# Grouped attention by pairs of heads, with late tiles of q projected between its steps, and norm squares added on VectorE

## The reference

```python
def rmsnorm_2(x, g):
    return x * lax.rsqrt(jnp.mean(x * x, axis=-1, keepdims=True) + EPS) * g

def attention_mixer(h, w_qkv, w_o, q_gain, k_gain, cos, sin):
    G = N_HEADS // N_KV_HEADS                       # 16 heads, 4 kv heads, HEAD_DIM 64
    q, k, v = jnp.split(h @ w_qkv, [N_HEADS * HEAD_DIM, (N_HEADS + N_KV_HEADS) * HEAD_DIM], axis=-1)
    q = apply_rope(rmsnorm_2(q, q_gain), cos, sin)  # over the 64 of a head
    k = apply_rope(rmsnorm_2(k, k_gain), cos, sin)
    def block(q_blk):                               # 128 queries
        s = jnp.einsum('bqkgd,bskd->bkgqs', q_blk, k) * HEAD_DIM ** -0.5
        p = jax.nn.softmax(s, axis=-1)
        return jnp.einsum('bkgqs,bskd->bqkgd', p, v)
    return lax.map(block, qb).reshape(Bsz, L, N_HEADS * HEAD_DIM) @ w_o
```

## Time and profile before

| what | value |
|---|---|
| median of 3 runs | 3399.99 us (3398.29 to 3401.54) |
| the profiled execution | 3402.33 us, span 3400.1 us |
| busy, of the span | PE 3083.2 (91%), DVE 1417.6 (42%), POOL 1525.8 (45%), ACT 720.1 (21%) |
| last products of the first k tile to first scores | 1781 to 1871 us |
| head loop, to the first product of `gq_out` | 1871 to 2039.6 us |
| a GEMM tile with no ones matmul, 24 products | 5.44 us |

### The profile page before, as it was taken

How to read it: one execution, slowest core, us unless ns; L and a number is a source line. 1 busy time by engine, 2 the same in 40 slices (tenths; PEclk the granted TensorE clock), 3 DMA queues, 4 the chain that set the end, 5 groups by cost and what they waited for, 6 DMA issues and landing times.

```text
span 3400.1 us, 38788 instructions
## 1 busy us (share of the span) xinstructions
PE 3083.2 (91%) x14739; PEld 2403.7 (71%) x14739; DVE 1417.6 (42%) x1983; ACT 720.1 (21%) x1069; POOL 1525.8 (45%) x926
## 2 busy tenths in 40 slices
PE   8897899999887999999989889999989777699998
PEld 7885898788634877788866437888867344478886
DVE  5675655111234047433344552332066666433311
ACT  2373222433232000111013551111011111011100
POOL 5441322444203655565543014666555444456663
PEclk9997999999898999999999999999989788899999
DMA  3110000222100245556541002333222000123331
GB/s 111 62 63 32 1 0 0 63 74 74 38 0 25 99 161 182 165 173 188 192 133 62 0 13 62 99 90 102 93 64 101 16 16 16 50 75 99 98 103 59
DMA packets 291644, 259.51 MB, mean 76 GB/s; under 512 B 6329, under 2 KB 263958, under 8 KB 291276
## 3 DMA queue, kind: packets, MB, share of 16 engines
q1 hardware_dynamic: 287840, 248.53, 23.4%
q0 software_dynamic: 2256, 6.55, 0.6%
q10 hardware_dynamic: 1436, 2.96, 0.2%
HBM read 255.92 MB, written 2.10 MB: 76 GB/s over the span
## 4 chain that ended last, share of the span: by engine, by line
PE 78%; DVE 9%; issue 4%; ACT 3%; POOL 2%; DVEq 2%; DMA 1%; POOLq 1%; ACTq 0%; SPq 0%
PE ps L487 19%; PE ps L488 19%; PE ps L489 18%; DVE cv L1881 2%; PE ps L1377 2%; PE ps L1357 2%; PE ps L1453 2%; PE ps L1150 1%; PE ps L1163 1%; PE ps L578 1%; PE ps L1260 1%; PE ps L1169 1%; PE ps L692 1%; DVE HN L598 1%; PE ps L1270 1%
## 5 line engine op out<-in xcount | busy, mean ns | idle before, releaser
L487 PE MATMUL ps<-HNH,spl 128*128 128x512 f32 (+1 forms) x2496 | 914.5, 366 | 61.3 <-DVE HNL L591 24.2
L661 POOL TENSOR_TENSOR spl<-raw,spl 128x1024 fp32r<-128x1024 f32 (+1 forms) x352 | 894.5, 2541 | 55.3 <-issue 5.5
L488 PE MATMUL ps<-HNL,spl 128*128 128x512 f32 (+1 forms) x2496 | 899.3, 360 | 0.0
L489 PE MATMUL ps<-HNH,spl 128*128 128x512 f32 (+1 forms) x2496 | 895.7, 359 | 0.0
L659 POOL CAST spl<-raw 128x1024 fp32r<-128x1024 f32 (+1 forms) x352 | 390.5, 1109 | 1055.0 <-PE ps L489 974.5
L487 PEld LDWEIGHTS ps<-HNH,spl 128*128 128x128 f32 x2496 | 480.2, 192 | 160.9 <-issue 58.6
L488 PEld LDWEIGHTS ps<-HNL,spl 128*128 128x128 f32 x2496 | 480.6, 193 | 72.6 <-issue 4.3
L489 PEld LDWEIGHTS ps<-HNH,spl 128*128 128x128 f32 x2496 | 479.4, 192 | 69.7
L487 PE MATMUL ps<-AFH,spl 128*128 128x512 f32 x528 | 212.8, 403 | 0.0
L489 PE MATMUL ps<-AFH,spl 128*128 128x512 f32 x528 | 205.8, 390 | 0.0
L488 PE MATMUL ps<-AFL,spl 128*128 128x512 f32 x528 | 205.8, 390 | 0.0
(11 more groups left out here) (419 smaller groups left out, 4348.9 us busy)
## 6 DMA issues: line engine op xcount, KB each, us to landing
adw<-in_ada_w SPq DMA_DIRECT2D x96, 512.0 KB, 6.2
raw<-in_w_in SPq DMA_DIRECT2D x44, 1024.0 KB, 5.2
raw<-in_ffn_w_up SPq DMA_DIRECT2D x88, 512.0 KB, 4.8
raw<-in_w_ffn_in SPq DMA_DIRECT2D x44, 512.0 KB, 5.0
raw<-in_ffn_w_down SPq DMA_DIRECT2D x16, 1408.0 KB, 6.4
raw<-in_hy_w_in SPq DMA_DIRECT2D x12, 1024.0 KB, 5.1
raw<-in_w_ffn_out SPq DMA_DIRECT2D x8, 1408.0 KB, 6.8
raw<-in_w_branch_dn SPq DMA_DIRECT2D x8, 1024.0 KB, 5.1
```

Of the source, the lines that this page charges most:

```text
L487: pe.matmul(dst, w[0], x[0], start=first, stop=False)
L488: pe.matmul(dst, w[0], x[1], start=False, stop=False)
L489: return pe.matmul(dst, w[1], x[0], start=False, stop=final)
L661: pool.tensor_tensor(lo, w, hi, ALU.subtract).then_inc(split_ready, 1)
```

## The change

It has two parts that meet in the attention stage.

Norms (u=1 to 6; the first one, `norm_first_pe`, is as before): ACT writes the squares of tiles 1 to 6 into PSUM banks 1 and 3 in turn, those of tile 0 and 7 into the two buffers of `NSQ`. DVE adds each of the six to `NSQ` 0 (`norm_add`, called from `add_residual` behind the residual of the next tile, the last one ahead of the last tile's). PE makes two ones matmuls in place of eight, behind the whole GEMM.

Attention: the weights come in the order k, v, q. Ahead of the scores stand the k and v tiles and two of q (`AHEAD` = 4). The loop is written out as 32 steps e = 4p+j: pair p of heads (2p, 2p+1), which share a tile of `QG`, and block j of 128 queries. In step e PE computes the scores of step e+2 (two matmuls, one in each half of the partitions, straight from `QG` and `KDUP`) and transposes the two blocks of step e; weighted stands once a pair, at the first step of the next, as eight matmuls that take the two heads' column halves in turn, into bank 6. Pairs 0 to 5 each hold one of the six late q tiles: twelve products in step 1 and twelve in step 2, into bank 7, the sum in step 3, the rotation in step 0 of the next pair. POOL stages nothing; `OG` is gone, for DVE takes `OGL` from PSUM pair by pair.

```diff
@@ norms @@
+                if u:
+                    if k in (3, 4, 5, 6):
+                        act.wait_ge(n_add, (KD - 2) * (u - 1) + k - 2)
+                    dst = NSQ[:, k // (KD - 1), 0:n] if k in (0, KD - 1) else ps[:, 1 + k % 2 * 2, 0:n]
+                    act.activation(dst, x(k), ACT.Square).then_inc(n_sq, 1)
...
-        def norm_after(pe, u):
-
-            return lambda t: norm_pe(pe, u, SEQ, range(t - 1, t)) if t else None
+        def norm_pe(pe, u):
+            pe.wait_ge(n_add, (KD - 2) * u)
+            pe.matmul(ps[:, 6, :], ones[:, :], NSQ[:, 0, 0:SEQ], start=True, stop=False).then_inc(n_sum, 1)
+            pe.wait_ge(n_sq, KD * (u + 1))
+            pe.matmul(ps[:, 6, :], ones[:, :], NSQ[:, 1, 0:SEQ], start=False, stop=True).then_inc(n_sum, 1)
+
+        def norm_add(dve, u, k):
+            dve.wait_ge(n_sq, KD * u + k + 1)
+            dve.drain()
+            x = NSQ[:, 0, 0:SEQ]
+            dve.tensor_tensor(x, x, ps[:, 1 + k % 2 * 2, :], ALU.add).then_inc(n_add, 1)
...
-            def add_residual(gm, gate=None, before=None):
+            def add_residual(gm, u, gate=None, before=None):
...
+                    if t == KD - 1:
+                        norm_add(dve, u, t - 1)
                     b = acc_in(dve, gm, 0, t)
...
+                    if 2 <= t < KD - 1:
+                        norm_add(dve, u, t - 1)
@@ POOL @@
-            pool_split(pool, gq_k)
-            pool_split(pool, gq_q)
-            pool_split(pool, gq_v)
-            pool.wait_ge(a_done, 10)
-            pool.wait_ge(a_dupc, KVH)
...
+            for gm in (gq_k, gq_v, gq_q):
+                pool_split(pool, gm)
@@ PE, attention @@
+            def q_part(n, bank, ks):
...
+                    if n < AHEAD:
+                        pe.wait_ge(acc_free[gm.buf(t)], gm.free(t))
+                    else:
+                        pe.wait_ge(a_done, n)
+                for k in ks:
+                    mm = products(pe, ps[:, bank, :], halves_of(gm, t, k), x_hn(k), k == 0, k == KD - 1)
...
+            def scores(e):
+                p, q = e // NT, e % NT
+                if q == 0:
+                    pe.wait_ge(a_done, FIRST_Q + p + 1)
+                if e >= 2:
+                    pe.wait_ge(a_e, 2 * (e - 1))
+                for s in range(2):
+                    x = slice(s * HD, (s + 1) * HD)
+                    mm = pe.matmul(ps[:, e % 2 * 2 + s, :], QG[x, p, q * P:(q + 1) * P], KDUP[x, p // 2, :], start=True, stop=True)
+                mm.then_inc(a_s, 1)
+
+            def turn_over(e):
+                for s in range(2):
+                    i = 2 * e + s
+                    pe.wait_ge(a_p, i + 1)
+                    if i >= 2:
+                        pe.wait_ge(a_tc, i - 1)
+                    for kt in range(NT):
+                        mm = pe.transpose(ps[:, 4 + s, kt * P:(kt + 1) * P], PB[:, e % 2, s, kt * P:(kt + 1) * P], ident)
+                    mm.then_inc(a_t, 1)
+
+            def weighted(p):
+                pe.wait_ge(a_tc, 2 * NT * (p + 1))
+                if p:
+                    pe.wait_ge(split_x, NT + KD + p)
+                for kt in range(NT):
+                    for s in range(2):
+                        x = slice(s * HD, (s + 1) * HD)
+                        mm = pe.matmul(ps[x, 6, :], VG[:, kt, p // 2 * HD:(p // 2 + 1) * HD], PTB[:, p % 2, s, kt, :],
+                                       start=kt == 0, stop=kt == NT - 1)
+                mm.then_inc(a_o, 1)
...
+                if n and j in (1, 2):
+                    q_part(n, 7, range(4 * j - 4, 4 * j))
+                if n and j == 3:
+                    qk_sum(n)
+                turn_over(e)
+                if j == 0 and p and late_tile(e - 1):
+                    qk_rot(late_tile(e - 1))
+            weighted(PAIRS - 1)
@@ ACT, attention @@
+            for e in range(STEPS):
+                p, j, n = e // NT, e % NT, late_tile(e)
+                if n and j == 2:
+                    q_in(n)
+                turned(e)
+                if n and j == 3:
+                    qk_rs(n)
+                if e + 2 < STEPS:
+                    exps(e + 2)
+                if j == 0 and p:
+                    heads_hi(p - 1)
@@ DVE, attention @@
+            for e in range(STEPS):
+                p, j, n = e // NT, e % NT, late_tile(e)
+                shares(e)
+                if e + 2 < STEPS:
+                    maxima(e + 2)
+                if n and j == 3:
+                    q_norm(n)
+                if j == 0 and p and late_tile(e - 1):
+                    rope(late_tile(e - 1))
+                if j == 1 and p:
+                    heads_lo(p - 1)
```

More of the change, by code:

```diff
@@ new lines, in v_turn_over @@
+            def v_turn_over(t):
+                taken(pe, gq_v, 0, t)
+                for c in range(NT):
+                    mm = pe.transpose(ps[:, 4 + t, c * P:(c + 1) * P], PTB[:, 0, 0, t, c * P:(c + 1) * P], ident)
+                mm.then_inc(sv_t, 1)
+            def scores(e):
[8 more added lines that the diff above has]
+                mm.then_inc(a_s, 1)
@@ new lines, in turned, with heads_hi @@
+            def turned(e):
+                p, q = e // NT, e % NT
+                if q == 0 and p >= 2:
+                    act.wait_ge(a_o, p - 1)
+                for s in range(2):
+                    act.wait_ge(a_t, 2 * e + s + 1)
+                    act.activation(PTB[:, p % 2, s, :, q * P:(q + 1) * P], ps[:, 4 + s, :].rearrange("p (k n) -> p k n", k=NT), ACT.Copy)\
+                        .then_inc(a_tc, 1)
+            def heads_hi(p):
+                act.wait_ge(a_o, p + 1)
+                act.activation(OGH[:, p, :], ps[:, 6, :], ACT.Copy).then_inc(a_oc, 1)
@@ new lines, in _ @@
+            q_in(0)
+            q_in(1)
+            qk_rs(0)
+            v_in(0)
+            qk_rs(1)
+            v_in(1)
+            k_both(0)
+            q_in(2)
+            k_both(1)
+            k_both(2)
+            qk_rs(2)
+            k_both(3)
+            q_in(3)
+            qk_rs(3)
+            exps(0)
+            exps(1)
+            for e in range(STEPS):
[7 more added lines that the diff above has]
+                    exps(e + 2)
+                if j == 0 and p:
+                    heads_hi(p - 1)
@@ new lines, in shares, with heads_lo @@
+            def shares(e):
+                dve.wait_ge(a_e, 2 * e + 2)
+                dve.reciprocal(asm[:, e % 2, 3, :], asm[:, e % 2, 2, :])
+                dve.drain()
+                for s in range(2):
+                    x = PB[:, e % 2, s, :]
+                    dve.tensor_scalar(x, x, asm[:, e % 2, 3, s:s + 1], None, ALU.mult).then_inc(a_p, 1)
+            def heads_lo(p):
+                dve.wait_ge(a_oc, p + 1)
+                dve.tensor_tensor(OGL[:, p, :], ps[:, 6, :], OGH[:, p, :], ALU.subtract).then_inc(split_x, 1)
@@ new lines, in _ @@
+            q_norm(0)
+            q_norm(1)
+            rope(0)
+            rope(1)
+            q_norm(2)
+            rope(2)
+            for t in range(2):
+                v_out(t)
+            q_norm(3)
+            maxima(0)
+            maxima(1)
+            rope(3)
+            for e in range(STEPS):
+                p, j, n = e // NT, e % NT, late_tile(e)
+                shares(e)
+                if e + 2 < STEPS:
+                    maxima(e + 2)
[5 more added lines that the diff above has]
+                    heads_lo(p - 1)
```

326 lines of the change are left out of this document (120 added, 206 removed).

## The result

The changed kernel takes 3305.03 us (median of 4 runs, 3296.41 to 3307.90) against 3399.14 for the one before; the ratio is 0.9719, 95% interval 0.9699 to 0.9739. That is 94 us less. Said were 3317, or 83 less, and a range of 3306 to 3344: the direction and the order of size held, the time lies 1 us under the range.

The account below looks back on a forecast made before the run. PE was taken as near full, not the softmax chain. Stage terms 38.7+0.9+2.9+130.8+29.2+3.5+1.4 gave 207.4 against 258.8 (−51.4); with the norms' −32, −83.4 and 3317 us, range 3306 to 3344.

Parts of the forecast that it names:

- The norms: Six norms: 36 ones matmuls go at 0.9 us each, 32 us less, range 26 to 33.
- Ahead of the first scores: Attention stage from first k tile to first scores: 38.7 us, plus 0.9 for a third rotation.
- A step and weighted: Attention loop: a step 2.5 us with scores in three slots; a pair's weighted 4.2 with nine slots of 0.43.
- the rope's wait: Late q tiles: PE waits at the next tile for the rope, 0.7 us, five times, 3.5.
- the two ends of the loop: Attention loop: 2.9 us for its filling and 1.4 for the last OGH and OGL.
- these stalls: Lower bound of the main case: no rope stall and no hand-overs, put at 9 us less.
- columns don't pair: Rival for weighted: only row halves pair, so 16 passes a pair, 24 us more, 3341; chance 0.24.
- nothing does: Rival for scores and weighted: nothing pairs steadily, 13.8 us more, 3354; chance 0.07.
- the third rival: Attention loop: PE waits at the rope or ACT's copies, up to 25 us, 3342 to 3390; chance 0.06.
- Steps that don't overlap: Rival for the loop: steps run as a chain of 7.6 us each, 78 more, 3478; chance 0.03.
- Dearer changes of shape: Rival for PE's 80 shape changes: at 0.4 us each 18 more, 3335; a twelfth of the main case's chance.
- DVE held up by POOL: Late tiles: POOL's weight splits slow DVE's rope and gain by at most 2.4 us a pair; hidden, otherwise 14.

Follow-up runs that it names:

- the second profile of the same kernel: The changed kernel, unaltered, run and profiled once more; 3304.17 us, ratio 0.9718.
- nothing side by side: Changed kernel with both scores of a step from one row half and both heads' weighted in one column half; 3360.13 us, ratio 0.9876.
- two and two: Changed kernel with a pair's weighted matmuls ordered two of the first head, two of the second, and again; 3304.90 us in a single run.
- both scores from one row half: Changed kernel with the second head's scores taken from the first head's row half; 3330.93 us, ratio 0.9788.

## Why the prediction came out as it did

**The norms: right.** Said 32, 33.4 in the trace. PE was full there, POOL did keep up at tiles of 5.4 to 5.5, and DVE's adds cost nothing. What was not in it is a wait of 2.0 at a ones matmul of `mix_out` that went too, hence 6.2 there and 5.1 to 5.4 elsewhere.

**Ahead of the first scores: nearly.** 38.7 and 0.9 said, 40.5 measured; the wait for the last rope is 2.5, not 0.3. Most of that is what the prediction looked for in the loop, DVE held up while POOL splits a weight slab: one operation of this rope began beside a split and took 2.63, where it takes 0.68 in the loop.

```profile
1804.61 2.34 POOL L674 TENSOR_TENSOR spl<-raw,spl 128x1024 fp32r<-128x1024 f32 x1
1804.87 2.63 DVE L2255 TENSOR_TENSOR QG<-QG,ropes 128x512 f32<-128x512 f32 x1
```

**A step and weighted: the pairing right, its extent wrong.** This is the step that failed. I took the scores of two heads at three slots and weighted at nine of sixteen: of two matmuls in different halves only the second pass of the one and the first pass of the other would share a slot, "each pass beside its neighbour". In fact both passes of the one share with both of the other, and they take two and eight. A step is 1870.38 to 1871.34 and on to 1872.40, 2.02 in place of 2.5; weighted with its change of shape 3.59 in place of 4.2. In the steady pair that is some 1.95+0.61 less; sum and rotation cost 1.92 and not 1.7, the rope's wait 1.18 and not 0.7, so a pair is 20.61 where 21.8+0.7 were said (the terms add up to 21.7, not 21.8). Over six pairs that makes 11 us, of which the projection ahead and the two ends of the loop gave some 4 to 5 back: 200.7 in place of 207.4. Of these 2.8 are the lower clock in the last pair and the last weighted, for the second profile of the same kernel has 197.8.

The slip was in reading. Four passes in the time of three were taken for what the array does at a border. They were what a wait left of it. The same stretch of the kernel before, with ACT:

```profile
1873.28 0.69 ACT L1766 ACTIVATE PB<-ps,asm 128x512 f32<-128x512 f32 x1 [2.82 <-DVE asm L2226]
...
1873.87 0.19 ACT L1766 ACTIVATION_READ_ACCUMULATOR PB<-ps,asm 128x1 f32 x1
```

Head 1's scores go into bank 0, which ACT releases when this exponential is done, at 1873.87+0.19 = 1874.06. Its first pass started at 1874.11, while head 0's last matmul was running (passes from 1873.78 and 1874.21). So it was the bank that had held it back, and only one pass of head 0 was left to share with. For matmuls that wait for nothing the experiments above show what the array does: they share whole slots. The lower bound of the range came from the same reading: it allowed for the stalls to vanish, but not for two and eight slots. (It put these stalls at 9, where the sum's own terms, 3.5 for the rope and 0.8 for hand-overs, make 4.3.) With two and eight the sum would have been 32×0.43+8×0.43 = 17 less, about 3300, and a range around it would have held the time.

**The rivals.** That columns don't pair, and that nothing does, were given 0.31 together; both are false, and the kernel with nothing side by side shows what the second would have cost: 3360, some 7 of it by the lower clock. (The 3390 of the third rival follows from no sum: 3354 and 25 are 3379.) Steps that don't overlap: no, PE waited 5.7 us in the whole stage for scaled P. Dearer changes of shape: from the last transpose's start at 1871.14 to the scores at 1871.34 are 0.20 where 0.11 is its own slot, 0.09; the first slot of scores and of weighted is 0.10 and 0.05 longer than 0.43. Together 0.19 and 0.14: the prices read before, which were right. DVE held up by POOL: DVE's scaling of a tile (L2247) took 0.744 to 0.753 all seven times from 1808 on, so nothing of it is seen in the loop, where none of the rope's or gain's operations met a split. Ahead of the scores it is there, as shown above.

**What the change consists of.** The late tiles between the steps, in which one would look for the gain, brought none that could be shown; the slots shared by pairs brought up to 47 of 58, and without the pairs 54 are lost, the lower clock included. I had the slots so in the sum, without saying that the interleaving could be left out.

**Spread.** The last 4 us of the difference are stretches that the change does not touch.

## What to carry to other kernels

Look for matmuls that use half of the rows or half of the columns and stand in a row on one half: put the partner for the other half directly behind each, and a full slot is saved for each couple of passes. One place further still worked where it was tried, for column halves in one run. Before a price is read from a rare event in a trace, ask which semaphore let it start when it did. When a part is said to fill idle time, take it out once: here the loop had little idle time left to fill. And when an experiment's total comes out as expected, look at its stretches with their granted clock: here the stage came out at 254.6 for 254 although the steady pairs had lost less than the sum said and the first pair more.

## What the runs showed of the hardware

- fp32 passes of two matmuls on disjoint row halves, or disjoint column halves, start 6 to 7 ns apart and take one slot of 0.43 together: 16 passes in 3.65, the same number of passes in one half 7.08. The Trainium skill, "TensorE: Matmul & The Clock Gate", Part 3, has such tiles start about 4 ns apart, measured on quarters; this trace agrees in kind for halves and fp32.
- With four matmuls of one half ahead of four of the other, the first of the second group started with the third of the first group, before the first group's fourth: 12 slots in place of 8 or 16. Three places behind the running matmul it had not been taken up. With two and two it was 8.
- A change from transposes to scores cost 0.09 of extra time at the border and 0.10 in the first slot, one from scores to weighted 0.09 and 0.05.
- DVE's L2255 from QG and `ropes` took 2.63 and 2.70 where it began beside POOL's L674 (1804.87, 1788.57), and 0.68 in the loop; each time it ended 0.55 after POOL did.
- With unpaired scores the granted clock was 0.50 over 16 us in which PE was busy for 16.00 (1811.33 to 1827.33 in "nothing side by side"; the same in "both scores from one row half").
- From the start of the same code's last weighted to the first product of `gq_out` it took 3.59 us (1962.45 to 1966.04) or 5.53 (1963.09 to 1968.62), where the window's granted clock was 1.00 or 0.82.
